# Compression MLP with its inputs as weights, one joint compressed softmax, and even column halves, in a hybrid decoder step on one core

## What is computed

```python
def compress_blocks(rows, pe, w1, w2):            # rows: raw keys or values, 2 heads of 128
    nc = (L - CMP_BLOCK) // CMP_STRIDE + 1        # windows of 32 rows, one every 16
    idx = CMP_STRIDE * jnp.arange(nc)[:, None] + jnp.arange(CMP_BLOCK)[None, :]
    blk = rows[:, idx] + pe[:, None, :]
    blk = jnp.swapaxes(blk, 2, 3).reshape(Bn, nc, NSA_KV_HEADS, CMP_BLOCK * HEAD_DIM)
    return jax.nn.gelu(blk @ w1) @ w2             # w1: 4096 x 256, w2: 256 x 128
# keys are rms-normed; then, per query head, with rel. bias b:
s = q @ kc + b;  p = masked_softmax(s, dist >= 0);  o_cmp = p @ vc
```

## Time and profile before

| | |
|---|---|
| median of three runs | 3329.32 us (3322.89 to 3329.73) |
| profiled execution | 3319.89 us, span 3317.8 us |
| TensorE busy | 3077.5 us (93%), 22,306 matmuls |
| VectorE, ScalarE, GpSimd busy | 1123.9, 846.1 and 130.5 us |
| granted TensorE clock, mean | 0.937 |
| HBM read and written | 247.79 MB and 16.50 MB |

### The profile page before, as it was taken

How to read it: one execution, slowest core, us unless ns; L and a number is a source line. 1 busy time by engine, 2 the same in 40 slices (tenths; PEclk the granted TensorE clock), 3 DMA queues, 4 the chain that set the end, 5 groups by cost and what they waited for, 6 DMA issues and landing times.

```text
span 3317.8 us, 54491 instructions
## 1 busy us (share of the span) xinstructions
PE 3077.5 (93%) x22306; PEld 2923.3 (88%) x22306; DVE 1123.9 (34%) x1646; ACT 846.1 (26%) x1485; POOL 130.5 (4%) x297
## 2 busy tenths in 40 slices
PE   6999999966687978869979999999999999999999
PEld 5999999956674546659969999999999999999999
DVE  3322134232321016422243443344423444334432
ACT  3222246331120024331132222222212222122221
POOL 0000000000000000000000110011000110001100
PEclk9999999877867979869989999999999999999999
DMA  5222222110004010113312222322232222222223
GB/s 182 89 97 87 89 83 83 36 80 0 1 28 162 27 51 1 51 41 104 110 64 83 89 79 83 98 89 89 74 89 97 89 89 76 89 96 89 89 75 128
DMA packets 91784, 261.34 MB, mean 79 GB/s; under 512 B 10018, under 2 KB 27202, under 8 KB 89458
## 3 DMA queue, kind: packets, MB, share of 16 engines
q1 hardware_dynamic: 87522, 243.91, 22.4%
q10 hardware_dynamic: 4032, 15.11, 1.3%
q0 software_dynamic: 144, 1.11, 0.1%
HBM read 247.79 MB, written 16.50 MB: 80 GB/s over the span
## 4 chain that ended last, share of the span: by engine, by line
PE 71%; DVE 4%; ACT 2%; issue 1%; DMA 0%; SPq 0%; DVEq 0%; ACTq 0%; PEldq 0%
PE ps L511 70%; PE ps L515 1%; DVE arena L1578 1%; DVE x_whole L1415 1%; DVE x_lo L1419 0%; DVE arena L1708 0%; DVE arena L1706 0%; ACT arena L1280 0%; DMA out_tail_g<-arena 0%; DVE arena L1591 0%; DMA arena<-in_w1c 0%; DVE arena L1654 0%; DMA arena<-in_ffn_w 0%; ACT arena L1259 0%; ACT x_hi L1039 0%
## 5 line engine op out<-in xcount | busy, mean ns | idle before, releaser
L511 PE MATMUL ps<-x_hi,w_hi 128*128 128x256 f32 (+1 forms) x4864 | 1015.3, 290 | 40.9 <-DVE w_lo L1424 23.2
L511 PE MATMUL ps<-x_hi,w_lo 128*128 128x256 f32 (+1 forms) x4864 | 1011.2, 289 | 0.0
L511 PE MATMUL ps<-x_lo,w_hi 128*128 128x256 f32 (+1 forms) x4864 | 1008.6, 289 | 0.0
L1424 DVE TENSOR_TENSOR w_lo<-w_whole,w_hi 128x1024 fp32r<-128x1024 f32 (+2 forms) x432 | 486.5, 1127 | 1462.8 <-ACT w_hi L1048 1454.7
L511 PEld LDWEIGHTS ps<-x_hi,w_hi 128*128 128x128 f32 x4864 | 789.9, 190 | 48.3 <-DVE w_lo L1424 24.1
L1048 ACT ACTIVATE w_hi<-w_whole 128x1024 fp32r<-128x1024 f32 (+2 forms) x432 | 422.8, 979 | 1582.1 <-PE ps L511 1580.4
L511 PEld LDWEIGHTS ps<-x_lo,w_hi 128*128 128x128 f32 x4864 | 788.5, 190 | 0.0
L511 PEld LDWEIGHTS ps<-x_hi,w_lo 128*128 128x128 f32 x4864 | 783.4, 189 | 0.0
L511 PE MATMUL ps<-arena 128*128 128x128 f32 (+19 forms) x2960 | 625.6, 386 | 156.2 <-DVE arena L1578 54.4
L511 PEld LDWEIGHTS ps<-arena 128*128 128x128 f32 (+8 forms) x2960 | 478.6, 234 | 287.9 <-issue 110.1
L511 PE MATMUL ps<-act_lo,w_hi 128*128 128x256 f32 (+1 forms) x1408 | 290.8, 287 | 0.0
(11 more groups left out here) (193 smaller groups left out, 1202.5 us busy)
## 6 DMA issues: line engine op xcount, KB each, us to landing
w_whole<-in_w_up SPq DMA_DIRECT2D x176, 512.0 KB, 3.4
w_whole<-in_w_proj SPq DMA_DIRECT2D x96, 512.0 KB, 3.6
w_whole<-in_w_dn SPq DMA_DIRECT2D x64, 384.0 KB, 3.1
w_whole<-in_w_dn SPq DMA_DIRECT2D x64, 320.0 KB, 2.9
w_whole<-in_w_o SPq DMA_DIRECT2D x32, 512.0 KB, 3.5
arena<-in_w1c SPq DMA_DIRECT2D x8, 1024.0 KB, 5.1
arena<-in_cache_kt SPq DMA_DIRECT2D x48, 128.0 KB, 2.6
arena<-in_x_t SPq DMA_DIRECT2D x4, 1088.0 KB, 12.0
```

The source lines that it names most:

```text
L511: return e.matmul(out, lhsT, rhs, start=start, stop=stop, skip_group_check=True)
L1424: e.tensor_tensor(wlo[h % 2][:, 0:n], raw[h % SLOTS][:, 0:n], whi_f[h % 2][:, 0:n], ALU.subtract).then_inc(w_lo, 1)
```

## The change

The diff below is cut to its core. In words:

- `halves` divides 544 columns into 272 and 272, in all products and in what reads their banks.
- Gates: `w_small` columns are the weights (128 columns are loaded, 32 of them are the gates), the tokens move. The result is gates x tokens; VectorE copies it and five transposes turn it to token-major.
- SP's order: tails are stored before the DeltaNet stage; the sample states are loaded after the page numbers, into the bias region; cached rows and the first 2 of 8 MB of `w1` are loaded during the sample part; `bfull` moves to SP.
- First layer: windows are the weights, with a step of 16 elements (two groups of 128 sample windows, one of 67 for prompt and positional rows), and 256 hidden columns of `w1` move. The result is window-major; VectorE copies it, and six transposes for each of keys and values turn it. The mirroring of the bias stands between the keys' and the values' first layer, and the keys' second layer inside the values' first layer.
- Compressed attention of the prompt: all 32 scores of four query blocks and eight heads first, one softmax over 128 x 992, with masked places set to a large negative number, then 32 transposes and eight copies.
- Sample group: compressed probabilities are spread to 128 places per group of four sequences, so that two products of 128 x 128 replace sixteen.

```diff
         def halves(x):
-            return x[:, 0:256], x[:, 256:NT]
+            return x[:, 0:HN], x[:, HN:NT]
...
             e.wait_ge(q_y, 4)
             e.wait_ge(s_cst, 16 * 7)
             pages = [e.value_load(ptab[0:1, q:q + 1], min_val=0, max_val=NPOOL - 1) for q in range(16)]
...
+            e.wait_ge(tails_out, 32)
+            e.dma_start(S_smp, A["state_gdn"]).then_inc(st_in, 16)
+            e.dma_start(O["gdn_sp"], W["S"]).then_inc(sp_out, 16)
...
+            e.wait_ge(kv_out, 16)
+            cached_rows(0)
+            first_layer(0)
+            e.dma_start(flip, A["flip"]).then_inc(flip_in, 16)
...
             e.wait_ge(g_act, GCS.end(1))
...
             e.dma_start(O["gdn_ss"], S_smp).then_inc(gdn_stored, 16)
...
+            e.wait_ge(sp_out, 16)
+            first_layer(1)
+            e.dma_start(w2, A["w2c"]).then_inc(w2_in, 16)
+            e.wait_ge(gdn_stored, 16)
+            src = bass.AP(table_dram.tensor, 0, [[1, P], [TAB, QH], [1, 512]])
+            e.wait_ge(t_out, 16)
+            e.dma_start(bfull, src).then_inc(bf_in, 16)
+            cached_rows(1)
+            for p in (2, 3):
+                e.wait_ge(units, U_CMP + 2 * p - 2)
+                first_layer(p)
...
+            for k in range(KC):
+                wh, wl = (w[0][:, 32 * k:32 * k + P] for w in (whi, wlo))
+                for q, (w, x) in enumerate(((wh, xhi), (wh, xlo), (wl, xhi))):
+                    start, stop = k + q == 0, k == KC - 1 and q == 2
+                    lo, hi = halves(x[:, k])
+                    mm(bank(4, HN), w, lo, start, stop)
+                    last = mm(bank(5, NT - HN), w, hi, start, stop)
+            last.then_inc(gates_mm, 1)
+            e.wait_ge(gates_row, 1)
             for t in range(5):
...
+                n = P if t < 4 else NS
+                last = tr(bank(6, 32, n, 32 * t), gates_t[:, P * t:P * t + n])
+            last.then_inc(gates_tok, 1)
...
             e.wait_ge(g_dve, GDS.end(1))
...
+            def first_layer(k, jh, lo=0, hi=16):
...
+                for jj in range(lo, hi):
+                    j = 16 * jh + jj
+                    w = w1p[jh][:, jj]
+                    for c in range(2):
+                        x = segs[k][:, 2048 * c + j:2048 * c + j + CS * (P - 1) + 1:CS]
+                        mm(bank(3 * k + c, 256).rearrange("p (c n) -> p c n", c=2), x, w, j == 0, j == CB - 1)
+                    x = rows_p[k][:, j:j + CS * (WP - 1) + 1:CS]
+                    last = mm(bank(3 * k + 2, 256, WP).rearrange("p (c n) -> p c n", c=2), x, w, j == 0, j == CB - 1)
...
+            e.wait_ge(seg_end, 1)
+            e.wait_ge(rows_in[0], 16 * 17)
+            first_layer(0, 0)
+            first_layer(0, 1)
+            e.wait_ge(units, U_CMP + 4)
+            e.sem_inc(cn_pe, 1)
+            e.wait_ge(bf_in, 16)
+            e.wait_ge(flip_in, 16)
+            for h in range(4):
+                last = mm(bank(3 + h), flip[:, 0:P], bfull[:, h])
+            last.then_inc(turned_pe, 1)
+            e.wait_ge(cn_c, 1)
...
+            e.wait_ge(turned, 1)
+            e.wait_ge(rows_in[1], 16 * 17)
+            first_layer(1, 0)
+            e.wait_ge(turned, 2)
...
+            hidden_turned(0)
+            first_layer(1, 1, 0, 8)
+            e.wait_ge(c_hid, 1)
...
+            first_layer(1, 1, 8, 16)
+            e.wait_ge(units, U_CMP + 8)
+            e.sem_inc(cn_pe, 1)
+            e.wait_ge(ck_sq, 1)
+            mm(bank(1, NCOL), ones, csq).then_inc(ck_n, 1)
+            hidden_turned(1)
...
             for i in range(4):
                 n = 7 + 8 * i
...
                 for h in range(QH):
...
+                    c = WS + 34 * (h // REP)
+                    last = mm(bank((4, 6)[i // 2], n, P, 248 * (i % 2) + NCP * h), kvq[:, N_A + h, P * i:P * i + P], kcT[:, c:c + n])
+            last.then_inc(ac_pe, 1)
+            e.wait_ge(v_act, 1)
+            e.wait_ge(cv_c, 1)
+            e.wait_ge(ac_dve, 2)
+            for h in range(QH):
+                for i in range(4):
+                    last = tr(bank(h, P, NCP, P * i), sC[:, i, h])
                 last.then_inc(ac_pe, 1)
...
-            for b in range(NB):
-                for g in range(G):
-                    n = 32 * b + 16 * g
-                    mm(bank(7, 16, P, n), vcS[:, G * b + g], s_CT[:, n:n + 16], n == 0, False)
+            for c in range(2):
+                mm(bank(7, P, P, P * c), vcS[:, c], s_CT[:, P * c:P * c + P], c == 0, False)
...
+            every = sC.rearrange("p i h c -> p (i h) c")
+            link(e.tensor_reduce(cmx, every, AX, ALU.max))
+            e.tensor_tensor(every, every, cmx.unsqueeze(2).broadcast_to([P, 4 * QH, NCP]), ALU.subtract).then_inc(ac_dve, 1)
+            e.wait_ge(ac_act, 1)
```

More of the change, by code:

```diff
@@ L537, in sum_squares @@
                 lo, hi = halves(sq)
-                mm(bank(banks, 256), ones, lo, first, last)
-                return mm(bank(banks + 1, NT - 256), ones, hi, first, last)
+                mm(bank(banks, HN), ones, lo, first, last)
+                return mm(bank(banks + 1, NT - HN), ones, hi, first, last)
             def group_norm(g):
@@ new lines, in hidden_turned @@
+            def hidden_turned(k):
+                e.wait_ge(cn_c, k + 1)
+                if k == 1:
+                    e.wait_ge(c_hid, 1)
+                for hc in range(2):
+                    for c in range(3):
+                        n = (P, P, WP)[c]
+                        last = tr(bank(6 + hc, n, P, P * c), hnat[k][0:n, c, P * hc:P * hc + P])
+                last.then_inc(ct_pe, 1)
+            e.wait_ge(g_act, GCS.end(1))
+            e.wait_ge(seg_end, 1)
+            e.wait_ge(rows_in[0], 16 * 17)
@@ new lines, in _ @@
+            first_layer(0, 0)
[8 more added lines that the diff above has]
+            e.wait_ge(cn_c, 1)
+            for h in range(4, QH):
+                last = mm(bank((7, 0, 1, 2)[h - 4]), flip[:, 0:P], bfull[:, h])
+            last.then_inc(turned_pe, 1)
@@ L1252, in _, with hidden @@
-            e.wait_ge(c_act, 5)
+            def hidden(k):
+                e.wait_ge(ct_pe, k + 1)
+                for hc in range(2):
+                    b = pebs[:, 2 * k + hc:2 * k + hc + 1]
+                    link(e.activation(b, bank(6 + hc, 1, P, NCOL - 1), ACT.Copy))
+                    last = e.activation(hid[:, k, hc], bank(6 + hc, NCOL), ACT.Gelu_apprx_tanh, bias=b)
+                last.then_inc(c_hid, 1)
+            e.wait_ge(turned_pe, 1)
+            for h in range(4):
+                last = e.activation(bfull[:, h], bank(3 + h), ACT.Copy)
@@ new lines, in _ @@
+            last.then_inc(turned, 1)
+            e.wait_ge(turned_pe, 2)
+            for h in range(4, QH):
+                last = e.activation(bfull[:, h], bank((7, 0, 1, 2)[h - 4]), ACT.Copy)
+            last.then_inc(turned, 1)
+            e.wait_ge(turned_pe, 3)
+            e.activation(biasB, bank(2, KEYS), ACT.Copy).then_inc(turned, 1)
+            hidden(0)
+            ln_exp()
+            e.wait_ge(ck_pe, 1)
+            e.activation(kcT, bank(0, NCOL), ACT.Copy)
+            e.activation(csq, bank(0, NCOL), ACT.Square).then_inc(ck_sq, 1)
@@ L1253, in _ @@
+            e.wait_ge(ck_n, 1)
+            rstd(crs, bank(1, NCOL), 1.0 / P, eps1).then_inc(ck_rs, 1)
+            hidden(1)
+            ln_exp()
             e.wait_ge(v_pe, 1)
```

318 lines of the change are left out of this document (139 added, 179 removed).

## The result

The changed kernel takes 3177.11 us (median of four runs, 3170.46 to 3180.89) against 3329.32 before: ratio 0.9545, 95% interval 0.9523 to 0.9567. Its profiled execution took 3180.89 us, with a span of 3178.7 us and a mean granted clock of 0.946.

| stage, from its first instruction to the next stage's | before, us | after, us | difference | my step |
|---|---|---|---|---|
| start and projection, to the gates | 641.2 | 638.8 | -2.4 | 0 (halves) |
| gates, to the first head sum | 41.8 | 14.1 | -27.7 | -27.7 |
| head norms and DeltaNet, to the first layer | 348.4 | 336.2 | -12.3 | -12.3 |
| first layer, to the prompt's attention | 209.4 | 128.8 | -80.6 | -79.9 |
| prompt's attention | 149.7 | 155.8 | +6.1 | 0 |

A forecast was written before the change was run, and what follows sets the result against it. TensorE was taken to bound the kernel, with 71% of the chain. Terms -27.7 + 0.5 - 92.7 - 5.6 + 0 = -125.5 from 3,319.9, plus 9.4 to the median, gave 3,204 us; own range 3,185 to 3,222, whole range 3,172 to 3,240.

The forecast's parts named there:

- 0 (halves): Dense stages: time about linear in columns, a pair of 272 + 272 costs the same 251 ns, so 0 us.
- Gates: Gates' products: 96 instructions in 12.0 us replace 39.7 us, saving 27.7 us; added copies and transposes counted at nothing.
- States and start of the first layer: Sample states loaded later lose 0 to 3 us, 0.5 taken; first layer starts 12.8 us earlier, without stores and weight load ahead.
- First layer to attention: First layer up to the prompt's attention: 129.5 us against 209.4, minus 79.9; joint softmax 9 us with handovers, transposes 7.
- 217 was my term: First layer: each of 384 instructions with 256 contiguous moving columns takes 217 ns, 83.3 us together.
- Rival (b): First layer: strided weight loads do not hide beside products; layer takes 152 us, time 3,273 us; chance 0.06.
- my upper bound of 213 and more: First layer: a strided load of 128 weights, as slow per element as the strided moving operand, takes 213 ns.
- the -5.6 predicted: Sample group: four matmul instructions replace 32, saving 6.1 us; two added multiplications cost about 0.5; minus 5.6 us.
- rival (a): Dense stages: even halves cost or gain 3 ns a pair, 28 us, giving 3,176 or 3,232; chance 0.13 each side.
- (c): Dense stages: moving columns taken in blocks of 32, so 272 costs what 288 does; 141 us more, 3,345 us; chance 0.06.
- the 2 ns that I had set as the sign of being wrong: Dense stages: pace stays 125.5 ns a matmul; the prediction is wrong if it moves by over 2 ns.
- The step to the median: Whole kernel: 9.4 us added because the median before, 3,329.3 us, lay that far above the profiled execution.

The follow-up runs named there:

- the three with parts added to it: Kernel before with even halves alone, 3311.01 us; with the gates' new products alone, 3297.46 us; with both together, 3277.35 us.
- two runs: Even halves alone in the kernel before, 3311.01 us, 14.3 less; 256 + 288 put back in the changed kernel, 3192.80 us, 14.4 above the even division.

## Why the prediction was right, and where it was off

**Gates: as predicted.** 27.7 us by the trace, 27.8 by the run that changes them alone.

**States and start of the first layer: as predicted.** -12.3 against +0.5 - 12.8. Of the 0 to 3 us that I allowed for the late states none was lost.

**First layer to attention: as predicted, 128.8 us for 129.5.** The terms that I listed add up to 128.8, not to the 129.5 that I wrote; the slip of 0.7 us changes nothing else. The parts fit too: the softmax leaves TensorE idle for 8.65 us (9), transposes and the last copy take 6.3 (7). The two matmul groups of the keys' layer, weights x moving columns:

```profile
L535 PE MATMUL ps<-arena 128*128 128x256 f32 x128 | 34.7, 395 | 1.5 <-DVE arena L1705 1.5
L535 PE MATMUL ps<-arena 128*67 128x256 f32 x64 | 19.5, 387 | 0.0
```

Against the earlier trace rows, where the moving operand had the step, 192 of them take 43.82 us; at full clock the pace is 216 to 222 ns, where 217 was my term. Rival (b) asked whether strided loads hide. They do, but only just: the load takes 217.7 ns, my upper bound of 213 and more, beside a product of 217. The trace has the edge of it: from 1,000 to 1,032.9 us an instruction with 67 inputs, whose load takes 115 ns, keeps 215.9 ns from start to start, and one with 128 inputs 219.4. The change moves the price of the step from the moving operand, where it was paid, to the weights, where a product of equal length covers it. Beside 128 moving columns in place of 256 the load would set the pace (an estimate: 128 columns are half of 217 ns). This is where the trace bears on the rule of the Trainium skill (SBUF — State Buffer, Specifications) that an access to a new 16-byte line each time is penalised: at full clock it agrees, 217.7 against 111.7 ns; at 0.50 the two loads hardly differ, 217.1 against 213.5.

**Sample group and prompt's attention: the direction was right, the size is not told apart from the clock.** The code of the prompt's attention is the same in all these kernels. Its stretch and that of the sample group's attention, in the kernel before, in the kernel before with even halves, and in the changed kernel:

```profile
1240.80:1390.50 149.70, 125.52 (x672) 97.59 (x672) 82.73 (x205) 62.51 (x200) 0.00 (x0) 0.89 0.01 1
1390.50:1446.90 56.40, 51.72 (x298) 45.27 (x299) 7.21 (x27) 8.51 (x22) 0.00 (x0) 0.53 0.22 73
```

```profile
1237.50:1395.10 157.60, 134.28 (x673) 104.42 (x673) 82.87 (x205) 62.64 (x200) 0.00 (x0) 0.82 0.01 2
1395.10:1448.40 53.30, 48.66 (x298) 42.39 (x298) 7.16 (x27) 8.51 (x22) 0.00 (x0) 0.56 0.23 77
```

```profile
1117.90:1273.70 155.80, 131.81 (x672) 102.40 (x672) 82.67 (x206) 62.64 (x200) 0.00 (x0) 0.84 0.01 1
1273.70:1319.70 46.00, 40.82 (x270) 34.97 (x270) 7.65 (x29) 8.52 (x22) 0.00 (x0) 0.61 0.26 91
```

VectorE's time is the same in all, TensorE's grows as the granted clock falls from 0.89 to 0.82. Over four executions with the old compression stage (before, and the three with parts added to it) the prompt's attention takes 149.7 to 157.6 us, mean 152.6; over the ten with the new one 148.4 to 155.8, mean 152.4. So the +6.1 us of the first table is scatter, not an effect of the change. In the same executions the sample group's attention takes 53.3 to 56.4 us with the old code, mean 54.9, and 45.0 to 49.4 with the new, mean 46.7. That is -8.2 for the -5.6 predicted, at granted clocks of 0.53 to 0.56 with the old code and 0.57 to 0.63 with the new where they were read; how the 2.6 us between divide into instructions and clock was not measured.

**Even halves: the term that was mis-sized.** I had 0, with 14 us a plausible shift; it is -14.3 and -14.4 us by two runs, and -2.4 - 11.9 in the table. The step that failed is "time is about linear in columns", and with it "six operand forms average out". It compared durations of two sizes, 284 and 298 ns, whose difference for 32 columns came near the mean pace; but the duration of an overlapped matmul is not its pace, and a pace for each size is not enough, since the same two sizes cost more than even halves in an up stretch and less in a down stretch. The four up stretches give some 9.5 us and the down stretches take 1.4 back; the rest of the 14 us lies, by difference, in the two projections. The group of after that answers to the earlier trace rows shows how little a duration tells:

```profile
L535 PE MATMUL ps<-x_hi,w_lo 128*128 128x272 f32 x4896 | 1009.5, 288 | 0.0
```

From start to start the trace of before has 117.8 ns for a 256 and 133.0 for a 288, 15.2, and in the odd up tiles 759.2 ns for six matmuls where the even ones have 747.5. That was a sign that the place of a tile counts, which a sum of columns can't give. Of rival (a)'s 28 us half came, on the side of the gain; (c), which would have made a 272 as dear as a 288, fell: 124.6 against 132.8 ns. The pace of the dense stages moved by 0.9 ns, under the 2 ns that I had set as the sign of being wrong.

**The step to the median.** I added 9.4 us, since the profiled execution of before lay that far under the median. It was at the low end of a scatter: in all, runs of before went from 3319.8 to 3331.5 us. The profiled execution of after lay 3.8 us over its median, at clock 0.946, where the shortest run had 0.950. So the point was 27 us too high for two reasons of equal size: 13.5 us of the sum (the halves; +6.1 and -4.8 us in the two attention stages nearly cancel), and 13.2 of this step. The measured 3177 us lie below the 3,185 to 3,222 that I gave the forecast itself, and inside the whole range only because that takes in rival (a). That they lie beside (a)'s 3,176 is luck: the halves gave half of that gain, and the step to the median, which no rival had, gave as much again.

**Open:** why the price of a pair of halves hangs on the operands, the tile and the order. No run has the compression stage alone; its 99 us are what the gates and the halves leave.

## What to carry to other kernels

In a stage where one engine never pauses, a nanosecond per instruction is the largest unknown: read the pace from start to start, by size, by position and by stage, and price a resize by a run of it in each stage: here one division won in one stage and lost in the next. When an access with a step can't be avoided, put it on the operand whose time is hidden, and check that what hides it is as long as the access. A stage whose clock moves between its levels shifts by several microseconds with no change in it, so set a term of such a stage against several executions, and don't carry one execution's distance from the median into a forecast.

## What the runs showed of the hardware

- A load of 128 fp32 inputs with a step of 16 elements took 217 ns at clock 1.00 and at 0.50; one of neighbouring elements took 112 at 1.00 and 213 at 0.50. The strided load doesn't follow TensorE's clock.
- In the run with 64 columns and strided weights TensorE shows no idle time from 990 to 1,020 us, and the granted clock was 0.50 throughout. In the values' layer it fell from 1.00 to 0.50 at 1,037 us, and there TensorE had been busy without a pause since 1,023.5 us, at the end with the 64-column products.
- The fastest of five divisions of 544 columns was the even one, by 14 to 84 us, though in the down stretches 256 + 288 was faster, 131.61 against 131.95 us. With even halves the order that alternates the banks was 13 us faster than three matmuls in a row into one bank; with 320 + 224 that order was not the faster one (3262.1 against 3254.0 us, one run).
